# Gate-up matrices of the middle experts in 4 MB transfers instead of 2 MB ones

## The chip, the core and the metric

The kernel runs on one core of a Trainium2 chip. The metric is the device time of one launch in microseconds (us). TensorE (PE) multiplies, VectorE (DVE) and ScalarE (ACT) do the element-wise work, GpSimd (POOL) some set-up, and SyncE (SP) issues nearly all transfers. The transfers run on the core's 16 DMA engines: each takes 8 of the 128 partitions' rows of a transfer, and a semaphore tells the consumer when all 16 are through.

## The reference

One step of a hybrid decoder: a mixer, then a mixture of 32 experts, of which each of the 264 tokens (256 of a prompt, 8 samples) uses 4. All data are float32. What matters here is the expert part:

```
def expert_block(args):
    tok, e = args
    xb = x_pad[tok]
    h = jnp.einsum('rd,df->rf', xb, w_gate_up[e]) + b_gate_up[e]
    gate = jnp.minimum(h[:, :D_FF], SWIGLU_LIMIT)
    up = jnp.clip(h[:, D_FF:], -SWIGLU_LIMIT, SWIGLU_LIMIT)
    glu = gate * jax.nn.sigmoid(gate * SWIGLU_ALPHA)
    return jnp.einsum('rf,fd->rd', (up + 1.0) * glu, w_down[e]) + b_down[e]
```

`w_gate_up[e]` is 1024 x 2048 (8 MB), `w_down[e]` is 1024 x 1024 (4 MB). Every weight is used once, so the 32 experts bring 403 MB through the DMA engines.

## The kernel before

The launch has two stages. The mixer takes roughly the first 290 us. After it come the experts, in 16 pairs, each expert with room for 64 tokens, so that the two experts of a pair share the PE's 128 columns or rows.

The weights go through a ring of 8 slots of 2 MB in SBUF (16 KB a partition), `ring` (slots 0 to 5) and `late_ring` (slots 6 and 7, whose memory is the mixer's until its end). One slot holds one chunk: a quarter of a gate-up matrix (256 rows, two neighbouring rows of 8 KB in each partition, i.e. one piece of 16 KB a partition) or half a down matrix (four neighbouring rows of 4 KB a partition, also 16 KB). The order of the chunks is a fixed list for each pair of experts. With the chunks numbered from 0:

- `HEAD`, chunks 0 to 7: gate-up of experts 0 and 1.
- `BODY`, 14 times, 12 chunks each (the first is 8 to 19, the second 20 to 31): four of gate-up of the pair's first expert, four of the down matrices of the pair before, four of gate-up of the second expert. In the texts they are c0 to c11 of a body; c4 to c7 are the down ones.
- `LAST`, chunks 176 to 191: eight gate-up chunks and eight of down, the last ones loaded in pieces of 1 MB and 512 KB.

SP walks through this list. Ahead of chunk n it waits until PE has used chunk n-8, whose slot it takes (`used`, L555), and issues the load (`load_chunk`, L467 to L489). The load adds 16 to the semaphore of its slot (`expert_in`) when it has landed. PE waits for that semaphore ahead of each gate-up chunk (L915), works on it and then adds 1 to `used` (L928); for the down chunks it waits for two slots at once (L944) and adds 2 at the end (L955). PE has other work between the chunks: it gathers the tokens of the next pair (L1006), turns the hidden values (L994) and scatters results (L1035, L1036). All of this is in program order on PE, so PE's wait for one chunk holds up everything behind it.

Which rows of the gate-up matrix lie in which partition is chosen by the rearrangement of `gu_w` (L441). The gathered tokens have to lie in the same order (`gather`, L1004 to L1008, steps through the columns of `normed` by 2) and so do the norm weights (`ffn_pairs`, L603).

Of the kernel before, what the change touches and what calls it, by code (L numbers as in the profile page):

```python
# [37 lines left out]
P = 128  # L38
# [170 lines left out]
def build(nc, ins, outs):  # L209
# [4 lines left out]
    with ExitStack() as ctx:  # L214
        def sem(name):
            return ctx.enter_context(nc.semaphore(name))
# [158 lines left out]
        state_in = [sem(f"state_in{s}") for s in range(4)]  # L375
        state_out = [sem(f"state_out{s}") for s in range(4)]
        expert_in = [sem(f"expert_in{s}") for s in range(RING)]
        stored, y_out = sem("stored"), sem("y_out")
        cleared, sq_done, rms_done, rstd_ready, rstd_turned, rstd_row_ready = (
            sem(n) for n in ("cleared", "sq_done", "rms_done", "rstd_ready", "rstd_turned", "rstd_row_ready"))  # L380
# [57 lines left out]
        TILES = ((0, P), (P, P), (2 * P, NS))  # L438


        gu_w = ins["w_gate_up"].rearrange("l e (k p i) f -> (l e) p k (i f)", p=P, i=2)  # L441

        dn_w = ins["w_down"].rearrange("l e (k p i) f -> (l e) p k (i f)", p=P, i=4)

# [8 lines left out]
        def chunk_number(r, chunks, p, c):  # L453

            if chunks is HEAD:
                return PASS * r + c
            return PASS * r + len(BODY) * (p - 1) + len(HEAD) + c

        def chunk_there(r, chunks, p, c, b=0):

            before = c if chunks is HEAD else len(HEAD) + b * len(BODY) + c
            whole = 16 * (PASS // RING) * r + 16 * (before // RING + 1)
            if chunks is HEAD:
                return whole
            return whole + 16 * len(BODY) // RING * (p - b - 1)

        def load_chunk(sp, chunks, p, c, b=0):  # L467

            j, part, k = chunks[c]
            s = chunk_slot(chunks, c, b)  # L470
            if part == "gu":
                e = 2 * (0 if chunks is HEAD else p) + j
                src = gu_w[bass.ds(e, 1), :, k, :].rearrange("a p f -> p (a f)")
                sp.dma_start(slot(s), src).then_inc(expert_in[s], 16)
                return
            e, h = 2 * (p - 1 + j) + k % 2, k // 2
            if chunks is not LAST:
                src = dn_w[bass.ds(e, 1), :, h, :].rearrange("a p f -> p (a f)")
                sp.dma_start(slot(s), src).then_inc(expert_in[s], 16)
                return  # L480


            final = c == len(LAST) - 1
            for i, n in [(i, 1) for i in range(4)] if final else ((0, 2), (2, 2)):
                for x in range(2):
                    to = chunk_slot(chunks, c - 1 + x, b)
                    src = dn_w[bass.ds(e - 1 + x, 1), :, h, i * D:(i + n) * D].rearrange("a p f -> p (a f)")
                    sp.dma_start(slot(to)[:, i * D:(i + n) * D], src).then_inc(
                        expert_in[to] if i == 0 else last_in[i - 1] if final else later_in[2 * j + h], 16)  # L489
# [4 lines left out]
        @block.sync  # L494
        def _(sp):
            w_in = ins["w_in"].rearrange("l (k p) n -> p (l k) n", p=P)
            w_pb = ins["w_pool_branch"].rearrange("l (k p) n -> p (l k) n", p=P)
            w_ret = ins["w_ret_branch"].rearrange("l (k p) n -> p (l k) n", p=P)
            w_out = ins["w_out"].rearrange("l (k p) n -> p (l k) n", p=P)

            for t in range(2):
                sp.dma_start(tok[:, t, :], x_prompt[0, t * P:(t + 1) * P, :]).then_inc(x_in[t], 16)
            sp.wait_ge(cleared, 2)
            sp.dma_start(tok[0:NS, 2, :], x_sample.rearrange("b s d -> (b s) d")).then_inc(x_in[2], 16)
            sp.dma_start(tok[NS:NS + NM, 2, :], meta).then_inc(x_in[2], 16)

            def mix_chunk(i):
                kind, c = CHUNKS[i]
                s = i % MIX_SLOTS
                if i >= MIX_SLOTS:  # L510
                    sp.wait_ge(tile_done, last_tile(i - MIX_SLOTS) + 1)
                dst = unit(8 + s)
                if kind == "in":
                    cols = PROJ[c] * P
                    src = w_in[:, :, cols:cols + 2 * P]
                    dst = dst.rearrange("p (k n) -> p k n", k=KD)
                elif kind == "pb":
                    src = w_pb[:, :, c * 512:c * 512 + 512]
                    dst = dst.rearrange("p (k n) -> p k n", k=PG)
                else:  # L520
                    src = (w_ret if kind == "ret" else w_out)[:, :, c * 256:c * 256 + 256]
                    dst = dst.rearrange("p (k n) -> p k n", k=KD)
                sp.dma_start(dst, src).then_inc(wmix_in[s], 16)

            for i in range(C_PB):
                mix_chunk(i)
                if i == 1:
                    sp.dma_start(mix_consts[:, :], ins["consts"][:, N_KEPT:]).then_inc(consts_in, 16)
                    sp.dma_start(consts[:, EARLY:], ins["consts"][:, EARLY:N_KEPT]).then_inc(consts_in, 16)
                if i in (MIX_SLOTS + 3, MIX_SLOTS + 5):  # L530
                    load_chunk(sp, HEAD, None, (i - MIX_SLOTS - 3) // 2)

            sp.wait_ge(o_s_ready, 1)
            for s in range(4):
                sp.wait_ge(state_out[s], 32)
            sp.wait_ge(stored, 16 * 3)
            for s in range(2, 4):
                load_chunk(sp, HEAD, None, s)
            for i in range(C_PB, len(CHUNKS)):
                mix_chunk(i)  # L540

            sp.wait_ge(dve_took, T_OUT - T_YB)
            for s in range(RING_EARLY, RING):
                load_chunk(sp, HEAD, None, s)
            for s in range(2):
                sp.wait_ge(tile_done, last_tile(len(CHUNKS) - MIX_SLOTS + 2 * s + 1) + 1)
                load_chunk(sp, HEAD, None, 4 + s)

            def stream(r, chunks, p, b=0):

                for c in range(len(chunks)):
                    if chunks is LAST and chunks[c][1] == "dn" and chunks[c][2] % 2 == 0:

                        continue
                    sp.wait_ge(used, chunk_number(r, chunks, p, c) - RING + 1)  # L555
                    load_chunk(sp, chunks, p, c, b)

            with sp.Fori(1, NPAIR - 1, 2) as p:
                for b in range(2):
                    stream(0, BODY, p + b, b)  # L560
            sp.wait_ge(passes_ready, 1)
            passes = sp.value_load(passes_i[0:1, 0:1], min_val=1, max_val=NPASS)
            stream(0, LAST, NPAIR - 1)
            with sp.If(passes > 1):
                with sp.Fori(1, NPASS) as r:
                    with sp.If(passes > r):
                        stream(r, HEAD, None)
                        with sp.Fori(1, NPAIR - 1, 2) as p:
                            for b in range(2):
                                stream(r, BODY, p + b, b)  # L570
                        stream(r, LAST, NPAIR - 1)
            sp.wait_ge(y_first_ready, 1)
            sp.dma_start(y_prompt[0, 0:P, :], normed[:, 0, :]).then_inc(y_out, 16)
            sp.wait_ge(y_s_ready, 1)
            sp.dma_start(y_sample.rearrange("b s d -> (b s) d"), normed[0:NS, 2, :]).then_inc(y_out, 16)
            sp.wait_ge(y_out, 16 * 3)
            sp.wait_ge(stored, 16 * 3)
            sp.wait_ge(ret_out, 16)
            for s in range(4):
                sp.wait_ge(state_out[s], 32)  # L580
# [3 lines left out]
        def _(pool):  # L584
# [12 lines left out]
            for b in range(4):  # L597
# [2 lines left out]
            pool.dma_start(w_router, ins["w_router"].rearrange("l (k p) e -> p (l k) e", p=P)).then_inc(misc_in, 16)  # L600
            pool.dma_start(b_router[:, :], ins["b_router"].broadcast_to([P, NE])).then_inc(misc_in, 16)

            pool.dma_start(ffn_pairs.rearrange("p (k i) -> p k i", i=2),  # L603
                           ins["norm_ffn"].rearrange("l (k p i) -> p (l k) i", p=P, i=2)).then_inc(ffn_in, 16)
            pool.dma_start(pool_sample[0, :, 0:PBUF - 1, :], state_pool[0, :, 1:PBUF, :]).then_inc(stored, 16)


# [66 lines left out]
        def _(pe):  # L674
# [228 lines left out]
            def use_gate_up(r, chunks, p, c, j, half, b=0):  # L903
# [4 lines left out]
                if half == 0:  # L908
                    if k % 2 == 0:
# [2 lines left out]
                            pe.wait_ge(x_second_ready, 2 * r + 1 + k // 2)  # L912
                        else:
                            pe.wait_ge(x_ready, 2 * GATHERS * r + e + 1 + j + k // 2)
                    pe.wait_ge(expert_in[s], chunk_there(r, chunks, p, c, b))  # L915

                order = [(i, n) for n in range(2) for i in range(2)] if k == KC - 1 else [(i, n) for i in range(2)
                                                                                          for n in range(2)]
# [79 lines left out]
            def gather(r, g, half, bank, part=None):  # L998
# [2 lines left out]
                if half == 0 and part != 1:  # L1001
                    pe.wait_ge(one_hot_ready, GATHERS * r + g + 1)
                for k in blocks:
                    d0 = k // 2 * 2 * P + k % 2  # L1004
                    for t in range(3):
                        last = mm(psum[:, bank + half, (k % 4) * P:(k % 4 + 1) * P],  # L1006
                                  normed[:, t, d0:d0 - k % 2 + 2 * P:2],
                                  one_hot[:, t].rearrange("p j c -> p (j c)"), start=t == 0, stop=t == 2)  # L1008
                if part != 0:
                    last.then_inc(gathered, 1)  # L1010
# [823 lines left out]
```

## Time and profile before

| | us |
|---|---|
| median of three runs | 1229.53 (1227.49 to 1230.05) |
| span of the profiled execution | 1228.2 |
| PE busy | 1184.3 (96%) |
| DVE / ACT / POOL busy | 291.6 / 144.8 / 46.3 |

The profiled execution is given by its span, the time from its first to its last instruction. It lies 1.3 us under the median of the runs. The page's slices show three stretches. Up to about 300 us the DMA engines carry 80 to 313 GB/s. From 340 us on they carry 384 to 431 GB/s, busy in every slice, until shortly before the end. The PE row is at 9 tenths nearly everywhere; this busy time includes the tails of overlapping matmuls and says little on slack, so the waits are read from the other views.

### The profile page before, as it was taken

The page shows a single profiled execution, that of the slowest core. Times are in us where ns is not written, and L with a number is a line of the kernel's source. Part 1 is how long each engine was busy: PE and PEld are TensorE (multiplying, and loading weights), DVE is VectorE, ACT ScalarE, POOL GpSimd, SP SyncE. Part 2 cuts the span into 40 slices and gives each one's busy share as a digit, 9 for nine tenths or more (in the row PEclk, how much of TensorE's full clock was granted, in tenths as well). Part 3 has the DMA queues.
Part 4 walks back from the last instruction along what each step waited for, and adds up shares of the span by engine and source line. Part 5 has one row for each costly group of instructions (what it writes and reads, how often), then busy time and mean ns, then how long its engine had stood idle before and what let it go on. Part 6 is the DMA issues. An engine that isn't in the chain of part 4 may idle for free.

```text
span 1228.2 us, 14689 instructions
## 1 busy us (share of the span) xinstructions
PE 1184.3 (96%) x5910; PEld 624.1 (51%) x5910; DVE 291.6 (24%) x663; ACT 144.8 (12%) x288; POOL 46.3 (4%) x82
## 2 busy tenths in 40 slices
PE   8999999999999999999989999999998999999996
PEld 6888678877443444444434434343443444444432
DVE  2233311223122122121213221223121222212212
ACT  2122111002101101000101010010100000000112
POOL 3023310000000000000000000000000000000000
PEclk9999999999999999999989999999998999999999
DMA  9752776474999999999999999999999999999995
GB/s 313 243 206 80 250 251 225 138 274 154 414 384 418 429 428 427 429 429 429 427 429 429 429 429 429 428 428 427 427 429 427 431 428 429 429 427 430 427 419 207
DMA packets 65886, 450.85 MB, mean 367 GB/s; under 512 B 4433, under 2 KB 35453, under 8 KB 40752
## 3 DMA queue, kind: packets, MB, share of 16 engines
q1 hardware_dynamic: 62416, 438.95, 86.6%
q0 software_dynamic: 3088, 10.77, 2.7%
q8 instruction: 27, 0.44, 0.1%
q10 hardware_dynamic: 344, 0.61, 0.1%
q14 instruction: 11, 0.09, 0.0%
HBM read 444.46 MB, written 6.08 MB: 367 GB/s over the span
## 4 chain that ended last, share of the span: by engine, by line
PE 70%; DMA 27%; DVE 1%; SPq 1%; issue 0%; ACT 0%; POOL 0%; DVEq 0%; POOLq 0%
DMA ring<-in_w_down 26%; PE psum L923 20%; PE psum L934 18%; PE psum L858 18%; PE psum L1006 5%; PE psum L994 2%; DMA ring<-in_w_in 2%; PE psum L1035 1%; PE psum L1036 1%; PE psum L741 0%; PE psum L1023 0%; PE psum L756 0%; PE psum L879 0%; PE psum L924 0%; DVE normed L1782 0%
## 5 line engine op out<-in xcount | busy, mean ns | idle before, releaser
L923 PE MATMUL psum<-ring,x_T 128*64 128x512 f32 x768 | 350.1, 599 | 0.6 <-DVE x_T L1612 0.3
L924 PE MATMUL psum<-ring,x_T 128*64 128x512 f32 x768 | 350.1, 599 | 0.0
L934 PE MATMUL psum<-ring,act_T 128*64 128x512 f32 x736 | 176.5, 634 | 24.7 <-DMA ring<-in_w_down 24.7
L923 PEld LDWEIGHTS psum<-ring,x_T 128*64 128x64 f32 x768 | 99.5, 137 | 190.8 <-issue 180.3
L858 PE MATMUL psum<-u_T,ring 128*128 128x264 f32 (+1 forms) x704 | 167.7, 393 | 2.0 <-DVE u_T L1492 1.2
L858 PEld LDWEIGHTS psum<-u_T,ring 128*128 128x128 f32 x704 | 131.0, 190 | 30.0 <-issue 4.8
L1705 DVE TENSOR_TENSOR hg<-psum,params 128x512 f32<-128x512 f32 x32 | 22.1, 691 | 436.7 <-PE psum L994 436.7
L934 PEld LDWEIGHTS psum<-ring,act_T 128*64 128x64 f32 x736 | 57.7, 145 | 126.5 <-issue 123.4
L1006 PEld LDWEIGHTS psum<-one_hot,normed 128*128 128x128 f32 x816 | 101.0, 196 | 39.2 <-issue 38.3
L923 PE MATMUL psum<-late_ring,x_T 128*64 128x512 f32 x256 | 118.2, 600 | 0.0
L924 PE MATMUL psum<-late_ring,x_T 128*64 128x512 f32 x256 | 118.2, 600 | 0.0
L1006 PE MATMUL psum<-one_hot,normed 128*128 128x128 f32 x816 | 111.2, 287 | 0.6 <-DVE one_hot L1592 0.6
L924 PEld LDWEIGHTS psum<-ring,x_T 128*64 128x64 f32 x768 | 99.5, 137 | 0.0
L1722 DVE TENSOR_TENSOR z_T<-z_T,psum 128x264 f32<-128x264 f32 x120 | 46.4, 425 | 126.9 <-PE psum L1036 122.1
L1297 ACT COPY h_raw<-psum 128x512 f32<-128x512 f32 x32 | 18.8, 587 | 379.9 <-PE psum L924 379.9
L923 PEld LDWEIGHTS psum<-late_ring,x_T 128*64 128x64 f32 x256 | 31.9, 136 | 56.5 <-issue 51.5
L1303 ACT ACTIVATE hs<-hg 128x512 f32<-128x512 f32 x32 | 20.2, 630 | 290.3 <-DVE hg L1708 290.3
L934 PE MATMUL psum<-late_ring,act_T 128*64 128x512 f32 x224 | 49.6, 595 | 0.0
L994 PEld LDWEIGHTS psum<-consts,h_raw 128*128 128x128 f32 x256 | 33.3, 209 | 26.4 <-issue 26.0
L1035 PEld LDWEIGHTS psum<-hot_T,out_hi 128*128 128x128 f32 x112 | 21.0, 187 | 45.4 <-issue 45.4
L1717 DVE SCALAR_TENSOR_TENSOR act_T<-hu,hs 128x512 f32<-128x512 f32 x30 | 20.8, 692 | 83.3 <-PE psum L934 76.7
L994 PE MATMUL psum<-consts,h_raw 128*128 128x128 f32 x256 | 39.8, 297 | 0.0
(265 smaller groups left out, 811.7 us busy)
## 6 DMA issues: line engine op xcount, KB each, us to landing
ring<-in_w_gate_up SPq DMA_DIRECT2D x96, 2048.0 KB, 27.3
ring<-in_w_down SPq DMA_DIRECT2D x42, 2048.0 KB, 31.1
late_ring<-in_w_gate_up SPq DMA_DIRECT2D x32, 2048.0 KB, 28.5
late_ring<-in_w_down SPq DMA_DIRECT2D x14, 2048.0 KB, 31.6
ring<-in_w_in SPq DMA_DIRECT2D x22, 1024.0 KB, 5.7
ring<-in_w_down SPq DMA_DIRECT2D x12, 1024.0 KB, 28.2
ring<-in_state_ret POOLq DMA_DIRECT2D x8, 512.0 KB, 7.4
out<-ring POOLq DMA_DIRECT2D x8, 512.0 KB, 4.5
```

The lines of the kernel that those rows point to most:

```text
L858: last = mm(o[:, 0:width], w[:, k, cols:cols + P], x[:, k, 0:width], start=k == 0, stop=k == nk - 1)
L923: mm(psum[0:CAP, 2 * j + n], x, gate, start=first, stop=final)
L924: last = mm(psum[CAP:P, 2 * j + n], x, up, start=first, stop=final)
L934: last = mm(psum[j * CAP:(j + 1) * CAP, 4 + n], hidden[:, j, 4 * h + i], w, start=h == 0 and i == 0, stop=h == 1 and i == 3)
L994: last = pe.transpose(psum[:, 6 + m // 4, (m % 4) * P:(m % 4 + 1) * P], h_raw[:, j, f0:f0 - m % 4 + 4 * P:4], ident)
L1006: last = mm(psum[:, bank + half, (k % 4) * P:(k % 4 + 1) * P], normed[:, t, d0:d0 - k % 2 + 2 * P:2], one_hot[:, t].rearrange("p j c -> p ...
L1035: mm(o, out_hi[:, c], hot_T[:, :], start=True, stop=False)
L1297: nc.scalar.copy(h_raw[:, j, 0:512], psum[:, 2 * j]).then_inc(raw_ready, 1)
L1303: A(hs[:, :, :], hg[:, :, :], ACT.Silu, scale=ALPHA).then_inc(silu_ready, 1)
L1705: V.tensor_tensor(hg, turned[:, :, 0], bias(e, 0), ALU.add).then_inc(gate_biased, 1)
L1717: V.scalar_tensor_tensor(hidden[:, j], hu, 1.0, hs, ALU.add, ALU.mult).then_inc(act_ready, 1)
L1722: V.tensor_tensor(y_T[:, d], y_T[:, d], psum[:, 6 + d % 2, 0:NT], ALU.add).then_inc(y_added, 1)
```

## The change

The gate-up chunks of the 14 bodies are loaded two at a time, except the first two. A transfer now has 4 MB, with four neighbouring rows (32 KB) in each partition, and fills two neighbouring slots. It is issued when PE has used both chunks that lay there before, and has one semaphore for the two slots (`pair_in`). PE waits for it ahead of the first chunk of the two and not ahead of the second. Of the 112 gate-up chunks in the bodies, 110 go in 55 such transfers; chunks 8 and 9 go in two 2 MB transfers into one `pair_in`. `HEAD`, `LAST` and the down matrices keep their transfers. Since the rows lie in another order, a gate-up chunk of `HEAD`, of `LAST` and chunks 8 and 9 are now pieces of 16 KB with a pitch of 32 KB in HBM; the gather steps by 4 columns instead of 2, and the norm weights follow. On SP the first two bodies now stand outside the loop.

```diff
@@ -375,6 +375,7 @@
         state_in = [sem(f"state_in{s}") for s in range(4)]
         state_out = [sem(f"state_out{s}") for s in range(4)]
         expert_in = [sem(f"expert_in{s}") for s in range(RING)]
+        pair_in = [sem(f"pair_in{q}") for q in range(RING // 2)]
             sem(n) for n in ("cleared", "sq_done", "rms_done", "rstd_ready", "rstd_turned", "rstd_row_ready"))
@@ -438,7 +439,7 @@
-        gu_w = ins["w_gate_up"].rearrange("l e (k p i) f -> (l e) p k (i f)", p=P, i=2)
+        gu_w = ins["w_gate_up"].rearrange("l e (k p i) f -> (l e) p k (i f)", p=P, i=4)
@@ -456,13 +457,34 @@
                 return PASS * r + c
             return PASS * r + len(BODY) * (p - 1) + len(HEAD) + c
+        TWO_BODIES = (NPAIR - 2) // 2
         def chunk_there(r, chunks, p, c, b=0):
-            before = c if chunks is HEAD else len(HEAD) + b * len(BODY) + c
-            whole = 16 * (PASS // RING) * r + 16 * (before // RING + 1)
+            before = 16 * (1 + TWO_BODIES + 2) * r
             if chunks is HEAD:
-                return whole
-            return whole + 16 * len(BODY) // RING * (p - b - 1)
+                return before + 16
+            if chunks is LAST:
+                return before + 16 * (1 + TWO_BODIES + 1 + c // RING)
+            return before + 32 + 8 * (p - b - 1)
+        def pair_there(r, p, c, b):
+            again = 1 if chunk_slot(BODY, c, b) == 0 else 0
+            return 16 * 2 * TWO_BODIES * r + 16 * (1 + BODY[c][0] + again) + 16 * (p - b - 1)
+        def slots_of_pair(s):
+            return ring[:, s * SLOT:(s + 2) * SLOT] if s < RING_EARLY else late_ring[:, (s - RING_EARLY) * SLOT:(s - RING_EARLY + 2) * SLOT]
+        def gate_up_rows(e, k):
+            return gu_w[bass.ds(e, 1), :, k // 2, k % 2 * SLOT:(k % 2 + 1) * SLOT].rearrange("a p f -> p (a f)")
+        def load_pair(sp, p, c, b):
+            j, _, k = BODY[c]
+            s = chunk_slot(BODY, c, b)
+            src = gu_w[bass.ds(2 * p + j, 1), :, k // 2, :].rearrange("a p f -> p (a f)")
+            sp.dma_start(slots_of_pair(s), src).then_inc(pair_in[s // 2], 16)
         def load_chunk(sp, chunks, p, c, b=0):
@@ -470,8 +492,7 @@
             if part == "gu":
                 e = 2 * (0 if chunks is HEAD else p) + j
-                src = gu_w[bass.ds(e, 1), :, k, :].rearrange("a p f -> p (a f)")
-                sp.dma_start(slot(s), src).then_inc(expert_in[s], 16)
+                sp.dma_start(slot(s), gate_up_rows(e, k)).then_inc(expert_in[s], 16)
                 return
             if chunks is not LAST:
@@ -552,10 +573,31 @@
                     if chunks is LAST and chunks[c][1] == "dn" and chunks[c][2] % 2 == 0:
+                    if chunks is BODY and chunks[c][1] == "gu":
+                        if chunks[c][2] % 2 == 0:
+                            sp.wait_ge(used, chunk_number(r, chunks, p, c + 1) - RING + 1)
+                            load_pair(sp, p, c, b)
+                        continue
-            with sp.Fori(1, NPAIR - 1, 2) as p:
+            def first_pair():
+                for c in range(2):
+                    sp.wait_ge(used, chunk_number(0, BODY, 1, c) - RING + 1)
+                    sp.dma_start(slot(c), gate_up_rows(2, c)).then_inc(pair_in[0], 16)
+            first_pair()
+            for c in range(2, len(BODY)):
+                if BODY[c][1] == "dn":
+                    sp.wait_ge(used, chunk_number(0, BODY, 1, c) - RING + 1)
+                    load_chunk(sp, BODY, 1, c)
+                elif BODY[c][2] % 2 == 0:
+                    sp.wait_ge(used, chunk_number(0, BODY, 1, c + 1) - RING + 1)
+                    load_pair(sp, 1, c, 0)
+            stream(0, BODY, 2, 1)
+            with sp.Fori(3, NPAIR - 1, 2) as p:
                 for b in range(2):
@@ -600,8 +642,8 @@
-            pool.dma_start(ffn_pairs.rearrange("p (k i) -> p k i", i=2),
-                           ins["norm_ffn"].rearrange("l (k p i) -> p (l k) i", p=P, i=2)).then_inc(ffn_in, 16)
+            pool.dma_start(ffn_pairs.rearrange("p (k i) -> p k i", i=4),
+                           ins["norm_ffn"].rearrange("l (k p i) -> p (l k) i", p=P, i=4)).then_inc(ffn_in, 16)
@@ -912,7 +954,10 @@
-                    pe.wait_ge(expert_in[s], chunk_there(r, chunks, p, c, b))
+                    if chunks is not BODY:
+                        pe.wait_ge(expert_in[s], chunk_there(r, chunks, p, c, b))
+                    elif k % 2 == 0:
+                        pe.wait_ge(pair_in[s // 2], pair_there(r, p, c, b))
                 order = [(i, n) for n in range(2) for i in range(2)] if k == KC - 1 else [(i, n) for i in range(2)
                                                                                           for n in range(2)]
@@ -1001,10 +1046,10 @@
                 if half == 0 and part != 1:
                 for k in blocks:
-                    d0 = k // 2 * 2 * P + k % 2
+                    d0 = k // 4 * 4 * P + k % 4
                     for t in range(3):
-                                  normed[:, t, d0:d0 - k % 2 + 2 * P:2],
+                                  normed[:, t, d0:d0 - k % 4 + 4 * P:4],
                 if part != 0:
```

SP, the load of c8 to c11 of a body inside the loop, before. `used` is the wait for the slot, `128x4096` is 16 KB a partition:

```order
L474 ISA [waits used]
L474 DMA ring<-in_w_gate_up 128x4096
L555 REGISTER_ALU
L474 ISA [waits used]
L474 DMA ring<-in_w_gate_up 128x4096
L555 REGISTER_ALU
L474 ISA [waits used]
L474 DMA late_ring<-in_w_gate_up 128x4096
L555 REGISTER_ALU
L474 ISA [waits used]
L474 DMA late_ring<-in_w_gate_up 128x4096
L555 REGISTER_ALU
```

The same place now. `128x8192` is 32 KB a partition:

```order
L487 ISA [waits used]
L487 DMA ring<-in_w_gate_up 128x8192
L579 REGISTER_ALU
L487 ISA [waits used]
L487 DMA late_ring<-in_w_gate_up 128x8192
L582 REGISTER_ALU
```

Four waits and four loads have become two and two. Each wait is now for the later of the two chunks whose slots are taken.

PE, first body, from the last matmuls of c8 into c9 (`expert_in1` is the semaphore of c9's slot), before:

```order
L924 MATMUL psum<-ring,x_T 64x512
L923 MATMUL psum<-ring,x_T 64x512
L924 MATMUL psum<-ring,x_T 64x512
L923 MATMUL psum<-ring,x_T 64x512 [waits hidden_took,expert_in1,out_split,hot_ready]
L924 MATMUL psum<-ring,x_T 64x512
L923 MATMUL psum<-ring,x_T 64x512
L924 MATMUL psum<-ring,x_T 64x512
```

The same place now:

```order
L969 MATMUL psum<-ring,x_T 64x512
L968 MATMUL psum<-ring,x_T 64x512
L969 MATMUL psum<-ring,x_T 64x512
L968 MATMUL psum<-ring,x_T 64x512 [waits hidden_took,out_split,hot_ready]
L969 MATMUL psum<-ring,x_T 64x512
L968 MATMUL psum<-ring,x_T 64x512
L969 MATMUL psum<-ring,x_T 64x512
```

The wait for the second chunk's own load is gone; the other waits of that instruction stay. PE, the same body, from the scatter inside c9 into c10, before:

```order
L1030 REGISTER_ALU
L1035 MATMUL psum<-hot_T,out_hi 128x264 [waits y_added]
L1036 MATMUL psum<-hot_T,out_lo 128x264
L1030 REGISTER_ALU
L1035 MATMUL psum<-hot_T,out_hi 128x264 [waits y_added]
L1036 MATMUL psum<-hot_T,out_lo 128x264
L923 MATMUL psum<-ring,x_T 64x512 [waits expert_in2,x_ready]
L924 MATMUL psum<-ring,x_T 64x512
L923 MATMUL psum<-ring,x_T 64x512
```

The same place now:

```order
L1075 REGISTER_ALU
L1080 MATMUL psum<-hot_T,out_hi 128x264 [waits y_added]
L1081 MATMUL psum<-hot_T,out_lo 128x264
L1075 REGISTER_ALU
L1080 MATMUL psum<-hot_T,out_hi 128x264 [waits y_added]
L1081 MATMUL psum<-hot_T,out_lo 128x264
L968 MATMUL psum<-ring,x_T 64x512 [waits pair_in1,x_ready]
L969 MATMUL psum<-ring,x_T 64x512
L968 MATMUL psum<-ring,x_T 64x512
```

Ahead of c10 PE now waits for `pair_in1`, the landing of c10 and c11 together; its line number moved with the diff and its work is the same.

## Rows read from the trace of the kernel before

**Rows 1.** windows: busy us (count) by engine, PEclk, DMA share, GB/s.

```profile
400.00:1130.00 730.00, 706.42 (x3500) 305.67 (x3499) 161.42 (x332) 67.77 (x127) 0.00 (x0) 0.98 1.01 428
1176.00:1196.00 20.00, 18.29 (x92) 7.16 (x90) 2.65 (x5) 3.14 (x5) 0.00 (x0) 1.00 1.01 421
1202.00:1208.00 6.00, 6.00 (x26) 2.40 (x25) 0.00 (x0) 0.00 (x0) 0.00 (x0) 1.00 1.02 408
```

**Rows 2.** critical chain: start us, length us, what; 394 to 503 us.

```profile
393.95 1.16 PE psum L994 x8
...
502.31 1.16 PE psum L994 x8
```

**Rows 3.** the same chain, 868 to 1112 us.

```profile
868.75 7.09 PE psum L934 x32
...
1044.93 8.78 PE psum L934 x32
...
1071.51 32.01 DMA ring<-in_w_down
1103.65 8.48 PE psum L934 x32
```

**Rows 4.** waits, 540 to 1130 us: total us, times, longest.

```profile
PE psum L934 <- DMA ring<-in_w_down: 23.0, 9, 4.0
```

**Rows 5.** one line (L474): its DMAs, issue to landing.

```profile
DMA to landing us min/median/max: 7.6/27.7/35.3
```

**Rows 6.** SP by time, 300 to 400 us: start, length, issues.

```profile
300.74 3.76 SPq L474 DMA_DIRECT2D ring<-in_w_gate_up  x2
...
311.42 3.77 SPq L474 DMA_DIRECT2D ring<-in_w_gate_up  x2
...
319.88 3.80 SPq L479 DMA_DIRECT2D ring<-in_w_down  x2
...
329.93 6.92 SPq L479 DMA_DIRECT2D late_ring<-in_w_down  x2
...
339.96 5.06 SPq L474 DMA_DIRECT2D ring<-in_w_gate_up  x2
...
355.08 0.33 SPq L474 DMA_DIRECT2D ring<-in_w_gate_up  x1
...
363.74 0.92 SPq L474 DMA_DIRECT2D ring<-in_w_gate_up  x2
...
373.62 0.91 SPq L474 DMA_DIRECT2D late_ring<-in_w_gate_up  x2
```

**Rows 7.** windows, 326 to 420 us.

```profile
326.00:360.00 34.00, 34.00 (x184) 16.12 (x184) 5.82 (x12) 2.98 (x5) 0.00 (x0) 1.00 1.00 421
...
362.00:364.00 2.00, 2.00 (x12) 0.83 (x9) 0.00 (x0) 0.00 (x0) 0.00 (x0) 1.00 0.39 164
```

**Rows 8.** SP by time, 1124 us on.

```profile
1125.52 4.59 SPq L474 DMA_DIRECT2D ring<-in_w_gate_up  x2
```

**Rows 9.** PE by time, 1186 to 1200 us; in brackets idle before.

```profile
1188.65 3.65 PE L934 MATMUL psum<-ring,act_T 128*64 128x512 f32 x16 [0.44 <-DMA ring<-in_w_down]
1193.53 3.65 PE L934 MATMUL psum<-ring,act_T 128*64 128x512 f32 x16 [1.23 <-DMA ring<-in_w_down]
1198.69 1.90 PE L934 MATMUL psum<-ring,out_sq 128*64 128x512 f32 x7 [1.50 <-DMA ring<-in_w_down]
```

**Rows 10.** windows: PE after its wait at 1103 us.

```profile
1103.00:1106.00 3.00, 2.35 (x6) 0.86 (x8) 0.00 (x0) 0.00 (x0) 0.00 (x0) 0.51 1.00 426
...
1186.00:1200.00 14.00, 10.83 (x53) 3.65 (x51) 1.50 (x2) 1.37 (x2) 0.00 (x0) 1.00 1.01 418
```

**Rows 11.** PE by time, 1103 us.

```profile
1103.65 1.98 PE L934 MATMUL psum<-ring,act_T 128*64 128x512 f32 x4 [2.78 <-DMA ring<-in_w_down]
```

**Rows 12.** groups of PEld (weight loads) by line, 540 to 1130 us.

```profile
L1006 PEld LDWEIGHTS psum<-one_hot,normed 128*128 128x128 f32 x480 | 59.7, 196 | 24.3 <-issue 24.3
L994 PEld LDWEIGHTS psum<-consts,h_raw 128*128 128x128 f32 x160 | 20.7, 209 | 16.2 <-issue 16.2
```

## The prediction

> **What bounds the kernel now.** I read the page's slices first, then windows of the expert stage, the chain of waits, and the issues of SP at the stage's start. The slices show that PE is at 9 tenths nearly everywhere and that the DMA engines are at 9 tenths from 340 us on, so busy shares don't decide. A window of 400 to 1130 us gives 428 GB/s with the DMA engines full [rows 1]. The chain decides. Early bodies are paced by PE: from 393.95 to 502.31 us two bodies pass, 54.18 us each, without a DMA in the chain [rows 2]. Later ones are paced by transfers: the first down matmuls of a body start at 868.75 and, four bodies on, at 1103.65, which is 58.72 us a body or 4.894 us a chunk (2.097 MB, so 428.5 GB/s) [rows 3]. PE could do a body in 54.2 us, so it waits: 23.0 us in nine waits between 540 and 1130 us, nearly all for a down chunk [rows 4]. So the end is set by this sum: when the stream of chunks starts, the time in which its queue is dry, bytes over rate, and the tail behind the last landing. PE matters only where it frees slots too late, or where it is late itself at the end.
>
> **Part 1: half the transfers for 110 chunks.** Every transfer costs something besides its bytes. From the rate by size of row [rows 1]: rows of 8 KB (1 MB a transfer) run at 421 GB/s, 2.491 us each, twice that is 4.981; less the 4.894 of one 2 MB transfer that leaves 0.087 us per transfer saved. Rows of 4 KB (512 KB) run at 408 GB/s, 1.285 us each, four are 5.140, less 4.894 leaves 0.246 for three, 0.082 each. I take 0.08. The change saves 55 of these, 4.4 us; five of the 55 fall into the start, counted in part 2, so 50 x 0.08 = 4.0 us here. Bounds: nothing is saved if the engines cut a 32 KB row in two (no row of the trace is that long in this queue); the most is 55 x 0.09 = 5.0 us.
>
> The Trainium skill (DMA: Bandwidth & Descriptors, "Anatomy of one DMA — SWDGE (gpsimd) path") gives a transfer 2.0 us fixed plus its bytes at 436 GB/s; were that paid in the queue, 55 fewer would save 110 us. The trace disagrees: it would make a body of twelve chunks 82 us, and it is 58.7 [rows 3]. The fixed part shows only where the queue is dry, as the 2.7 us of part 2. The same page ("Why small descriptors are slow (HBM only)") speaks of about 3 cycles per packet; by our estimate from its 850 MHz that is 28 ns for the eight packets of an engine, 1.5 us for 55 transfers, against 4.4 by the rows, and the sum would end near 1229.3.
>
> **Part 2: at the start the pairs come later.** Here SP is held by PE: the queue is nearly dry while PE uses chunks 0 to 15. A load issued into a dry queue lands after 7.6 us [rows 5], that is 4.9 of its own and 2.7 before. So I replay with: landing = the later of (landing before it + own time) and (issue + 2.7 + own time). Own time is 4.89, for a pair 9.71 (9.79 - 0.08). Issue times stand in [rows 6], where the last of a row's issues is start + length - 0.33. The slots' release by PE is the same, but a pair is issued at the later of its two times.
> Before: chunks 8 and 9 (issued 300.74, 304.16) land at 308.3, 313.2; 10 (311.42) at 319.0; 11 to 14 every 4.89 to 338.6; 15 (336.51) at 344.1; 16 to 19 to 363.7; 20 (363.74) at 371.3, so the queue is dry for 2.7 us, seen as 164 GB/s in the window from 362 us [rows 7]; 21 at 376.2; 22 and 23 (373.62) at 381.2 and 386.1.
> Now: 8 and 9 the same; 10 and 11 issued together at 314.85, landing 327.3 (before 323.9); 12 to 15 at 346.9; 16 and 17 issued at 344.69, landing 357.1; 18 and 19 at 355.08, landing 367.5; 20 and 21 at 363.74, queued, landing 377.2; 22 and 23 landing 386.9.
> That is 0.8 us later than before. The dry 2.7 us at 362 us absorb most of it. Other traffic holds the stream at 421 instead of 428.5 GB/s from 326 to 360 us [rows 7], 34 x 0.018 = 0.6 us; before it hid in part in dry time, now it has less to hide in. So +0.8 to +1.4 us, and I take 1.3. Later no pair is late: loads land a median 27.7 us after issue [rows 5], over five chunks, and a pair gives up one chunk of that. PE has chunks in hand throughout this stretch (chunk 10 is used after 344.69), so it isn't held.
>
> **Part 3: PE waits for two chunks where it waited for one.** Behind each such wait stand all of PE's gathers, turns and scatters, then ACT and DVE, and SP's next loads. While PE is 4.5 us a body ahead this only moves the waits: now it waits up to about 2 us ahead of c8, c10, c0 and c2, and reaches the down chunks late by about what it would have waited. It counts only in the last body, whose end PE carries into the tail. There, c9 ends at 1129.8 (1125.52 + 4.59 - 0.33) [rows 8]. The first down chunks of that body had landed at 1103.52 (1071.51 + 32.01) [rows 3]; c11 lands six chunks on, at 1132.9, and with the gain of parts 1 and 2 at 1130.2. So c10 starts 0.4 us later than before. From there PE has slack 0.44 + 1.23 + 1.50 = 3.2 us, its waits ahead of the last down pieces [rows 9]; less the 0.4 that is 2.8 us. After the last of these waits PE runs through to its end. So the gain can't pass 3.2 us whatever the DMA engines save, and 2.8 is my value for this limit.
>
> **Part 4: the rest.** The gather reads weights with a step of 4 columns. A weight load with step 2 is 196 ns, the step-4 loads of L994 are 209 [rows 12]; at worst 13 ns x 48 = 0.6 us of PE a body, hidden by its 4.5 us, and 0.3 us in the last expert's 24 gathers; if the two operands explain the difference, nothing or a little less. I take 0. Rows of 16 KB at a pitch of 32 KB for the 18 single gate-up chunks in `HEAD`, `LAST` and the first body: no row shows this; I take 0, and 1% of 18 x 4.9 us would be 0.9 either way. SP issues 55 fewer; each is 0.33 us under a queue that is full, so 0. The norm weights' load is far ahead of its use, 0.
>
> **Sum.** DMA: -4.0 + 1.3 = -2.7 us. PE's limit: -2.8. So 1228.2 becomes 1225.5 as a profile. The median of the runs is 1.3 above that profile: 1229.53 - 2.7 = 1226.8 us.
>
> **Rivals.**
> A, the row is cut: the engines move 32 KB as two packets and pay per packet. Then only the coarser start is left, +1.3, and 55 semaphores saved at most 0.5: 1230.4. For it: the saving in part 1 is read from smaller rows, and no row excludes it. Against: the rule held from 4 to 16 KB with one constant.
> B, PE's clock: after a wait of 2.78 us [rows 11] the granted clock fell to the lower level, 1.2 GHz (0.51 in the window from 1103) [rows 10], and the 32 down matmuls took 8.5 to 8.8 us instead of 7.1 [rows 3], 1.5 to 1.7 us. Waits of 0.44 to 1.50 did not do this: clock 1.00 from 1186 to 1200 [rows 10]. The new waits of about 2 us lie between. If both in the last body (c8, c10) cost 1.7, PE is 3.4 later, over its 2.8 of slack by 0.6, and instead of the gain the end is at 1229.5 - 2.7 + 3.4 - 0.1 = 1230.1. One such loss gives about 1228.4.
> C, slower: 32 KB rows run slower. Each engine then reads longer rows, 32 KB apart instead of 16. Place: all 110 chunks, 538 us. From 0.5% on (428.5 down to 426.3 GB/s, a pair over 9.84 us) it eats the 2.7; at 1% it costs 5.4 on top of the start's 1.3: 1236.2. For it: nothing shown, rates rise with the row (408, 421, 428). That rise is what speaks against it.
>
> **Numbers.** Forecast 0.66, A 0.13, B 0.12, C 0.09. About 0.2% (2.5 us) is what a measurement of this kernel can tell from no change. The forecast's own spread is 1225.3 (limit of PE, one us of scatter) to 1228.3 (0.05 per transfer, start 1.7), so it lies half over that bound: 0.43 of its 0.66 is faster, 0.22 the same, 0.01 slower. A and B are the same mostly, with 0.04 faster and 0.03 slower between them, C slower or the same. Together faster 0.47, same 0.42, slower 0.11. The range is 1225.0 to 1230.7: it holds A and B and leaves C out.
>
> **What would show it.** In the profile after: 55 gate-up issues of 4096 KB; down starts later than 700 us spaced 58.4 us (58.72 - 4 x 0.08) instead of 58.72, the clearest sign for part 1 (58.7 would be A, more would be C); no 164 GB/s slice at 362 us; PE's waits for `in_w_gate_up` no longer near zero, about the same total; waits ahead of the last down pieces near 0.5 us in total instead of 3.2. I am wrong if the spacing doesn't shrink, if the queue goes dry beyond 390 us, or if the spacing shrinks and the end does not follow.

## The result: 4.5% slower

| kernel | median us (lowest to highest) | ratio to before, 95% interval |
|---|---|---|
| before | 1229.79 (1227.49 to 1230.77), 4 runs | |
| changed | 1284.12 (1282.75 to 1286.19), 4 runs | 1.0447 (1.0435 to 1.0460) |

The forecast was 1226.8 us. The changed kernel is 54 us slower. The head of its page gives the profiled execution:

```profile
span 1282.5 us, 14402 instructions
PE 1264.3 (99%) x5910; PEld 711.7 (55%) x5910; DVE 292.9 (23%) x663; ACT 146.0 (11%) x288; POOL 46.2 (4%) x82
```

PE was 96% busy and is now 99% busy, with 80 us more busy time in the same number of matmuls (5910). The answers to [rows 4], PE's waits from 300 us to the end (total us, times, longest):

```profile
PE psum L979 <- DVE out_lo L1731: 0.8, 1, 0.8
PE psum L968 <- DVE x_T L1657: 0.3, 1, 0.3
```

Not one of PE's waits is for a transfer. They were 23.0 us in the middle stretch alone. So the bound has changed sides: the transfers wait for PE. The window that answers to the first of [rows 1] (engines as there):

```profile
400.00:1130.00 730.00, 729.85 (x3344) 352.91 (x3344) 158.56 (x325) 66.04 (x121) 0.00 (x0) 1.00 0.99 417
```

PE is busy for 729.85 of 730 us and the transfers run at 417 instead of 428 GB/s, because slots come free later. The issues by line, with the size and the median us from issue to landing, show that the transfers arrive sooner after their issue than before, not later:

```profile
ring<-in_w_gate_up SPq DMA_DIRECT2D x41, 4096.0 KB, 14.7
...
late_ring<-in_w_gate_up SPq DMA_DIRECT2D x14, 4096.0 KB, 14.5
```

There are 55 transfers of 4096 KB, as intended, and a landing takes 14.7 us where a single chunk took 27.7 [rows 5]: the queue is short. The chain, by the first of each body's turns of the hidden values (L1039 is L994 before; start, length):

```profile
410.00 1.16 PE psum L1039 x8
...
469.72 1.16 PE psum L1039 x8
...
529.43 1.16 PE psum L1039 x8
```

A body takes 59.7 us, all of it PE. It was 54.18 us where PE paced it and 58.72 where the transfers did [rows 2, 3]. Where the 5.5 us come from stands in the groups of PE's weight loads, which answer to [rows 12] (us busy, mean ns | idle before):

```profile
L1051 PEld LDWEIGHTS psum<-one_hot,normed 128*128 128x128 f32 x816 | 195.1, 329 | 39.2 <-issue 38.3 <-DVE one_hot L1637 0.9
...
L1039 PEld LDWEIGHTS psum<-consts,h_raw 128*128 128x128 f32 x256 | 33.3, 209 | 26.4 <-issue 26.0 <-ACT h_raw L1344 0.4
```

and in the matmuls of the same line, now:

```profile
L1051 PE MATMUL psum<-one_hot,normed 128*128 128x128 f32 x816 | 205.3, 403 | 0.6 <-DVE one_hot L1637 0.6
```

before:

```profile
L1006 PE MATMUL psum<-one_hot,normed 128*128 128x128 f32 x816 | 111.2, 287 | 0.6 <-DVE one_hot L1592 0.6
```

The gather's weight loads take 329 ns instead of 196, its matmuls 403 instead of 287. There are 48 of each in a body: 48 x 0.116 = 5.6 us. The turns' loads, whose step is 4 in both kernels, have not moved. The 133 ns between the two loads are more than PE pays, since the records of neighbouring loads overlap: the 816 loads are busy for 195.1 us now, 239 ns each, and were busy for 101.0 us, 124 ns each, which is 115 ns apart. The chain says the same. Twelve matmuls of the gather, before and now:

```profile
398.70 1.61 PE psum L1006 x12
```

```profile
414.75 3.00 PE psum L1051 x12
```

That is 1.39 us for twelve, 0.116 each. Below, the lengths of loads are given as the profile has them; what PE pays is read from the chain.

The 54 us are not 14 bodies at 5.5 us. The first down matmuls of the first, the fourth and (now) the last body, before and now (the last one before is at 1103.65 in [rows 3]):

```profile
356.51 7.02 PE psum L934 x32
...
519.05 7.02 PE psum L934 x32
```

```profile
371.19 7.02 PE psum L979 x32
...
550.33 7.02 PE psum L979 x32
...
1155.45 7.02 PE psum L979 x32
```

14.7 us are lost ahead of the first body's down matmuls, 16.6 in the three bodies behind them, which PE paced before too, and 20.5 in the last ten; 2.5 us come behind them. In the bodies that the transfers had paced at 58.7 us a body loses only about 1.0. Eight of the 20.5 us are one block on PE that both kernels have: 16 matmuls of the biases with short waits for DVE between them (5.8 us from 824 us on, L1078) and, behind them, about four us at the lower clock, 1.2 GHz (granted 0.50 from 828 to 832 us). Before, the body with this block took 62.6 us and the next one 54.9, so the two passed in the time of the transfers; now nothing takes it up.

### The profile page after: what moved, and what is told of

Its sections match the earlier page's. It is cut to its first block, busy times and chain, and to the rows that moved or that the text cites. A ratio compares the mean times of both kernels' runs of the same rounds, so it can differ in the third digit from the quotient of the medians.

```text
span 1282.5 us, 14402 instructions
## 1 busy us (share of the span) xinstructions
PE 1264.3 (99%) x5910; PEld 711.7 (55%) x5910; DVE 292.9 (23%) x663; ACT 146.0 (11%) x288; POOL 46.2 (4%) x82
## 4 chain that ended last, share of the span: by engine, by line
PE 97%; DVE 1%; ACT 0%; issue 0%; DVEq 0%
PE psum L968 35%; PE psum L900 18%; PE psum L979 17%; PE psum L1051 16%; PE psum L1039 3%; PE psum L1080 2%; PE psum L1081 1%; PE psum L969 1%; PE psum L1068 0%; PE psum L783 0%; PE psum L1078 0%; PE psum L798 0%; DVE normed L1827 0%; PE psum L771 0%; PE psum L770 0%; PE psum L762 0%
## 5 line engine op out<-in xcount | busy, mean ns | idle before, releaser
L1051 PEld LDWEIGHTS psum<-one_hot,normed 128*128 128x128 f32 x816 | 195.1, 329 | 39.2 <-issue 38.3
L1051 PE MATMUL psum<-one_hot,normed 128*128 128x128 f32 x816 | 205.3, 403 | 0.6 <-DVE one_hot L1637 0.6
L979 PE MATMUL psum<-ring,act_T 128*64 128x512 f32 x736 | 163.2, 596 | 0.0
L979 PEld LDWEIGHTS psum<-ring,act_T 128*64 128x64 f32 x736 | 50.8, 137 | 94.7 <-issue 92.9
L1767 DVE TENSOR_TENSOR z_T<-z_T,psum 128x264 f32<-128x264 f32 x120 | 46.5, 426 | 127.9 <-PE psum L1081 122.1
L1039 PEld LDWEIGHTS psum<-consts,h_raw 128*128 128x128 f32 x256 | 33.3, 209 | 26.4 <-issue 26.0
L1039 PE MATMUL psum<-consts,h_raw 128*128 128x128 f32 x256 | 39.8, 297 | 0.0
## 6 DMA issues: line engine op xcount, KB each, us to landing
ring<-in_w_gate_up SPq DMA_DIRECT2D x41, 4096.0 KB, 14.7
```

Source lines behind the costliest of these rows:

```text
L979: last = mm(psum[j * CAP:(j + 1) * CAP, 4 + n], hidden[:, j, 4 * h + i], w, start=h == 0 and i == 0, stop=h == 1 and i == 3)
L1039: last = pe.transpose(psum[:, 6 + m // 4, (m % 4) * P:(m % 4 + 1) * P], h_raw[:, j, f0:f0 - m % 4 + 4 * P:4], ident)
L1767: V.tensor_tensor(y_T[:, d], y_T[:, d], psum[:, 6 + d % 2, 0:NT], ALU.add).then_inc(y_added, 1)
```

## The experiments

Theory G: the loss is the gather, whose weight loads read the tokens with a step of 4 elements. Rival T: the loss is the 4 MB transfers, which come late or run slowly.

**The gather's step alone, in the kernel before.**

```diff
-                    d0 = k // 2 * 2 * P + k % 2
+                    d0 = k // 4 * 4 * P + k % 4
-                                  normed[:, t, d0:d0 - k % 2 + 2 * P:2],
+                                  normed[:, t, d0:d0 - k % 4 + 4 * P:4],
```

> The kernel before with one edit: the gather reads the tokens' columns with a step of 4 instead of 2. Rows and transfers stay as before, so the experts get the columns of each token in a wrong order; the work and its amount are the same. Theory G (the loss of 54 us is the gather's weight loads): the weight loads of the gather go from 196 to about 329 ns and its matmuls from 287 to about 403, a body takes PE about 59.9 us instead of 54.2, PE waits for no transfer, and the time is 1280 to 1288 us. Theory T (the loss is the 4 MB transfers, which come late): the time stays at 1228 to 1231 us.

Measured: 1285.30 us, ratio 1.0460 (1.0444 to 1.0476). The weight loads:

```profile
L1006 PEld LDWEIGHTS psum<-one_hot,normed 128*128 128x128 f32 x816 | 195.0, 328 | 39.2 <-issue 38.3 <-DVE one_hot L1592 0.9
...
L994 PEld LDWEIGHTS psum<-consts,h_raw 128*128 128x128 f32 x256 | 33.3, 209 | 26.4 <-issue 26.0 <-ACT h_raw L1299 0.4
```

PE's waits from 300 us on:

```profile
PE psum L934 <- DVE out_lo L1686: 0.8, 1, 0.8
PE psum L923 <- DVE x_T L1612: 0.3, 1, 0.3
```

This is the whole loss, with the transfers of before. Theory T falls.

**The changed kernel with the old step.** The same two lines the other way round.

> The changed kernel with one edit: the gather steps by 2 again, so the columns of each token are in a wrong order for its weight rows; everything else is as changed, with 55 transfers of 4 MB. Theory G: the gather's weight loads are back at 196 ns, PE waits for transfers again, and the time is what parts 1 and 2 of the prediction gave, 1225.5 to 1228.5 us, with 58.4 us a body where the transfers are the bound. Theory T: 1280 us or more. A mixed case, in which the coarse transfers cost something by themselves: 1230 to 1240 us.

Measured: 1225.83 us, ratio 0.9973 (0.9962 to 0.9983), faster than before. PE's waits from 300 us on:

```profile
PE psum L968 <- DMA ring<-in_w_gate_up: 26.1, 21, 1.7
PE psum L968 <- DMA late_ring<-in_w_gate_up: 6.1, 6, 1.1
PE psum L979 <- DVE out_lo L1731: 0.9, 1, 0.9
```

PE waits for transfers again, but in 27 short waits of at most 1.7 us ahead of gate-up pairs instead of a dozen up to 4.0 us ahead of down chunks: part 3 of the prediction as it was written. Two bodies of its chain:

```profile
925.96 7.04 PE psum L979 x32
...
1042.83 7.04 PE psum L979 x32
```

That is 58.43 us a body, with the gather of before, against 58.73 for the same two bodies of the kernel before.

**Both orders with the tokens packed.** ACT writes each block of 128 columns densely; the gather then reads with step 1. In the changed kernel (the other has `h=4, i=2`):

```diff
-                A(normed[0:n, t], banks((4, 6, 0)[t], 2)[0:n], ACT.Copy, ...)
+                A(normed[0:n, t].rearrange("n (h i p) -> n h i p", h=2, i=4),
+                  banks((4, 6, 0)[t], 2)[0:n].rearrange("n (h p i) -> n h i p", h=2, i=4),
+                  ACT.Copy, ...)
...
-                                  normed[:, t, d0:d0 - k % 4 + 4 * P:4],
+                                  normed[:, t, k * P:(k + 1) * P],
```

> The changed kernel, but ACT writes the normalised tokens so that the 128 columns of one gather block lie next to each other (three instructions that read PSUM with a step of 4 and write densely), and the gather reads them with step 1. Outputs are the reference's. Theory G: weight loads of the gather at 190 ns or less, the time 1225.0 to 1228 us, under the kernel before. Theory T: 1280 us or more.

> The kernel before with the same packing of the normalised tokens, for its own order of rows (ACT reads PSUM with a step of 2), gather with step 1, 2 MB transfers. Outputs are the reference's. The transfers are its bound, so a slightly faster gather gives little: 1228 to 1230 us by both theories. It is the base against which after_packed shows what the 4 MB transfers are worth: theory of part 1 says after_packed is 2 to 3.5 us below it.

Measured: after_packed 1225.49 us, 0.9967 (0.9955 to 0.9979); before_packed 1229.00 us, 0.9998 (0.9989 to 1.0007). The gather's loads in after_packed:

```profile
L1050 PEld LDWEIGHTS psum<-one_hot,normed 128*128 128x128 f32 x816 | 95.9, 192 | 39.2 <-issue 38.3 <-DVE one_hot L1638 0.9
```

The chain of after_packed, the first down matmuls of three bodies:

```profile
925.48 7.04 PE psum L979 x32
...
984.00 7.04 PE psum L979 x32
...
1042.33 7.04 PE psum L979 x32
```

and of before_packed:

```profile
926.66 9.53 PE psum L934 x32
...
985.38 8.78 PE psum L934 x32
...
1044.13 8.78 PE psum L934 x32
```

That is 58.43 us a body (116.85 for two) against 58.74 (117.47): four pairs save 0.31 us, 0.08 us each, the price of part 1. The transfers of after_packed in the same window as above:

```profile
400.00:1130.00 730.00, 696.93 (x3499) 298.13 (x3497) 162.33 (x334) 67.69 (x127) 0.00 (x0) 0.99 1.00 431
```

431 GB/s, where the kernel before has 428.

**The order of the rows with single transfers.**

```diff
-                src = gu_w[bass.ds(e, 1), :, k, :].rearrange("a p f -> p (a f)")
+                src = gu_w[bass.ds(e, 1), :, k // 2, k % 2 * SLOT:(k % 2 + 1) * SLOT].rearrange("a p f -> p (a f)")
```

on the packed kernel in the new order (`i=4` in `gu_w` and `ffn_pairs`).

> Rows in the new order (four neighbouring rows a partition), but every gate-up chunk in its own 2 MB transfer of 16 KB pieces at a pitch of 32 KB; the tokens packed, gather with step 1. Outputs are the reference's. If the gain of after_packed over before_packed (3.5 us) comes from fewer, longer transfers (the 0.08 us per transfer of part 1), this kernel is at 1228 to 1230 us with 58.7 us a body. If it came from the order of the rows itself, it is at 1225 to 1226 us. If pieces at a 32 KB pitch were slower by 1%, it would be at 1234 us.

Measured: 1227.44 us, 0.9987 (0.9978 to 0.9996). Its bodies:

```profile
925.29 9.83 PE psum L934 x32
...
984.02 7.09 PE psum L934 x32
...
1042.75 8.78 PE psum L934 x32
```

58.73 us on average, as with the old order, so pieces of 16 KB at a pitch of 32 KB are not slower. That its median lay 1.6 us under before was not expected, so the three were run again side by side:

> The packed kernel with the old order of rows and 2 MB transfers once more, on one chip with the next two, since the gains of order_2mb_packed (ratio 0.9987) and before_packed (0.9998) were measured in different calls. Expected 0.9995 to 1.0000 of the kernel before: its body is paced by transfers at 58.7 us.

> The new order of rows with 2 MB transfers once more. If the order of the rows is worth nothing, it equals before_packed_again within 0.1%; if it is worth the 1.6 us seen, it lies 1 us or more below it.

> The new order of rows with 55 transfers of 4 MB once more. If the fewer transfers are what gains (0.3 us a body, 58.4 instead of 58.7), it lies 2 to 4 us below both others; if the order of rows carries half of it, 1 to 2 us below order_2mb_packed_again.

Measured: 1228.26 us, 0.9995 (0.9986 to 1.0004); 1227.49 us, 0.9989 (0.9980 to 0.9998); 1224.28 us, 0.9967 (0.9955 to 0.9979). The 4 MB transfers are worth 3.2 to 4.0 us against the other two. Between the first two lie 0.8 us (1.6 in the runs before), with overlapping intervals and bodies of the same length. The new order came out lower both times; whether the order of the rows is itself worth this much stays open.

**How the price depends on the step.** The kernel before with step 3 and step 8 in the gather (`d0 = k * 64` and `d0:d0 + 3 * P:3`; `d0 = k` and `d0:D:8`).

> The kernel before with the gather's weight loads at step 3 (384 columns of which every third is read; data wrong, amount of work the same). Theory L (a load slows by the number of 16-byte lines it touches per element: 1 element per line is slow, 2 and more are not): step 3 has 4 elements in 3 lines, so the load lies between 196 (step 2) and 329 ns (step 4), about 240 to 290. If it is a threshold at step 4: 196. If any step over 2 is slow: 329.

> The kernel before with the gather's weight loads at step 8 (data wrong). Theory L: every element is in a line of its own from step 4 on, so the load stays at about 329 ns and the time at about 1285 us. If the cost grows with the bytes passed over: about 600 ns and well over 1350 us.

Measured, one run each: 1237.09 and 1287.11 us. The loads at step 3:

```profile
L1006 PEld LDWEIGHTS psum<-one_hot,normed 128*128 128x128 f32 x816 | 146.5, 260 | 39.2 <-issue 38.3 <-DVE one_hot L1592 0.9
```

and at step 8:

```profile
L1006 PEld LDWEIGHTS psum<-one_hot,normed 128*128 128x128 f32 x816 | 198.7, 333 | 39.2 <-issue 38.3 <-DVE one_hot L1592 0.9
```

With 192 ns at step 1 (after_packed), 196 at step 2 and 328 at step 4, the series is 192, 196, 260, 328, 333. The Trainium skill (SBUF — State Buffer, "Specifications (TRN2)") gives SBUF lines of 16 bytes, of which an access has to hit each at least twice to run at full speed. By 4-byte elements the steps 1, 2, 3, 4 and 8 touch 1/4, 1/2, 3/4, 1 and 1 line per element, and the measured series agrees: step 2 has two hits a line, step 4 one. So a load is nearly free of the step up to half a line per element, and from one line on it no longer grows. At step 3, PE hardly waits for transfers (total us, times, longest):

```profile
PE psum L934 <- DMA ring<-in_w_down: 2.6, 2, 1.5
```

The first turns of two bodies in its chain:

```profile
402.07 1.16 PE psum L994 x8
...
458.93 1.16 PE psum L994 x8
```

A body takes PE 56.86 us, 2.7 us more than at step 2 (48 x 0.056, by the matmuls, whose mean is 343 ns). That is less than the 4.5 us by which PE was ahead, and still the launch is 8 us longer (1237.09 against 1229.06). The landings in the two traces say where it is lost: the first down chunk of the second body, number 24, lands at 399.8 instead of 393.9 us, and from there to the end the transfers stay 6 to 8 us behind. In that first stretch SP waits for PE to free the slots, so there PE's time is not covered.

**Why L994 misled.** The turns of the hidden values as plain matmuls, and in another kernel the turns with step 1:

```diff
-                    last = pe.transpose(psum[...], h_raw[:, j, f0:f0 - m % 4 + 4 * P:4], ident)
+                    last = mm(psum[...], h_raw[:, j, f0:f0 - m % 4 + 4 * P:4], ident, start=True, stop=True)
```

```diff
-                                        h_raw[:, j, f0:f0 - m % 4 + 4 * P:4], ident)
+                                        h_raw[:, j, m * P:(m + 1) * P], ident)
```

> The kernel before, with the eight turns of the hidden values per expert (L994, step 4 in h_raw) as plain float32 matmuls against the identity instead of transposes. This is why the 209 ns of L994 misled the prediction: in transposes a step-1 load is 143 ns (L1023), so step 4 adds 66, and in plain matmuls step 1 is 190. If the price of step 4 belongs to the plain form, the loads of L994 go from 209 to about 329 ns. If it depends on the tile that is read (h_raw against normed), they go to 190 to 210. The whole time stays near 1230 us, since PE has slack there.

> The kernel before, with the turns of L994 reading h_raw with step 1 (data wrong). If the step was the reason for 209 ns, the loads of L994 fall to about 143 ns, the value of other transposes with step 1. If not, they stay at 209. The time stays at 1228 to 1230 us, transfers being the bound.

Measured, one run each: turn_plain 1275.57 us, turn_step1 1228.33 us. Weight loads of turn_plain:

```profile
L994 PEld LDWEIGHTS psum<-consts,h_raw 128*128 128x128 f32 x512 | 121.9, 328 | 26.0 <-issue 26.0
```

and of turn_step1:

```profile
L994 PEld LDWEIGHTS psum<-consts,h_raw 128*128 128x128 f32 x256 | 27.4, 141 | 26.6 <-issue 26.0 <-ACT h_raw L1299 0.7
```

The same tile and the same step, 209 ns as a transpose and 328 as a plain matmul; with step 1 the transpose loads in 141. In the chain, the turns of one expert (eight blocks of 128 x 128) as plain matmuls and as transposes with step 1:

```profile
401.80 3.93 PE psum L994 x16
```

```profile
416.14 1.02 PE psum L994 x8
```

Eight transposes with step 4 take 1.16 us [rows 2]. So in PE's time step 4 costs a transpose (1.16 - 1.02) / 8, about 0.017 us, where it costs a matmul of the gather 0.116. A plain float32 matmul is moreover two loads and two matmuls (x512 where the transposes were x256), so each of the two pays for the step. The expectation for turn_plain had the load right and the time wrong: 46.5 us were lost because the count doubled too, which I had not reckoned with, and PE's slack of 4.5 us a body was gone.

## Why the prediction was wrong

**The step that failed is in part 4:** "A weight load with step 2 is 196 ns, the step-4 loads of L994 are 209; at worst 13 ns x 48 = 0.6 us of PE a body, hidden by its 4.5 us." The measured term is 133 ns in the load's record, 0.116 us of PE a matmul, and 5.5 us a body in the spacing of the chain: over the 4.5 us by which PE was ahead. PE paces every body at 59.7 us. The 209 ns are those of a transpose, the 196 those of a plain matmul; I compared across two kinds. The trace of before has step 1 for the same kind as L994 (gated values, dense):

```profile
L1023 PEld LDWEIGHTS psum<-consts,gated 128*128 128x128 f32 x48 | 5.8, 143 | 0.8 <-issue 0.8
```

143 against 209 ns says that the step does lengthen a load, by 66 ns, and that would have been the warning. It isn't the price either. In PE's time the 66 ns of a transpose are 17, by turn_step1, and 48 x 0.017 = 0.8 us would have looked covered as well; the gather, in the plain form, pays 116. Why the plain form pays so much more isn't shown. None of the rows that I read had a plain matmul with a step over 2, and one was needed.

The cover was wrong too. The 4.5 us a body are there only in the bodies that the transfers pace; 31 of the 54 us were lost before these. And step3_only, whose 2.7 us a body are well inside the 4.5, lost 8 us. So the term was mis-sized, and what was to hide it hides less than I said.

The rule of the Trainium skill quoted with the series above says the same of steps 2 and 4. It names no size. It was the rule against this change, and the prediction should have weighed it.

**Part 1 was right.** A transfer saved is worth 0.08 us: 58.43 against 58.74 us a body where the transfers are the bound. The engines move a 32 KB row as one packet, as the packet count of the changed kernel's page shows:

```profile
DMA packets 57965, 450.84 MB, mean 352 GB/s; under 512 B 3553, under 2 KB 34573, under 8 KB 39872
```

The page of before counts 65886. The difference is 7921, and 55 transfers fewer, of 128 rows and 16 semaphore packets each, are 7920. So rival A falls, and with 431 GB/s so does C, a slower rate.

**Part 2 was right in kind.** The windows of after_packed that answer to the 164 GB/s of [rows 7]:

```profile
360.00:362.00 2.00, 2.00 (x12) 0.49 (x8) 0.00 (x0) 0.00 (x0) 0.00 (x0) 1.00 1.20 508
362.00:364.00 2.00, 2.00 (x17) 1.85 (x16) 0.44 (x1) 0.00 (x0) 0.00 (x0) 1.00 0.76 328
364.00:366.00 2.00, 2.00 (x16) 1.26 (x16) 2.00 (x5) 0.79 (x2) 0.00 (x0) 1.00 1.09 459
```

The dry stretch at 362 us is mostly filled: 328 GB/s in the slice that had 164. For the size of the part the landings in the traces of after_step2 and of before can be compared, which have the same gather. The pair of chunks 22 and 23 lands at 389.2 us where chunk 23 had landed at 388.2, and the first down chunk behind it at 394.2 instead of 393.9. So the start cost 0.3 to 1.0 us, where 1.3 were forecast. By chunk 168, in the last body, the transfers are 3.2 us ahead: 3.5 us gained over 48 pairs, 0.07 each, which bears out part 1.

**Part 3 was right in kind; its limit was too low.** The waits moved from the down chunks to the gate-up pairs. The end of after_packed (PE by time):

```profile
1182.22 3.65 PE L979 MATMUL psum<-ring,act_T 128*64 128x512 f32 x16
...
1186.77 7.09 PE L979 MATMUL psum<-ring,act_T 128*64 128x512 f32 x32
...
1194.96 3.65 PE L979 MATMUL psum<-ring,out_sq 128*64 128x512 f32 x16 [1.10 <-DMA ring<-in_w_down]
```

Of the 3.2 us of waits ahead of the last down pieces [rows 9] only 1.10 are left there, and none in after_step2, where PE runs through to its end; 0.5 were forecast. The forecast for parts 1 to 3, -2.7 us, measured -3.4 (after_step2) to -4.5 us (after_packed_again) against before; the second contains the step-1 gather. Both pass the 3.2 us that I had called the most that is possible, and the 2.8 that I took. In after_step2 c11 lands at 1129.5 us, not at 1130.2, so c10 starts at 1129.7 us and not 0.4 us later than before: the 0.4 that I took off the 3.2 were not there. Rival B, a falling clock, is not seen: PEclk is 0.99 in the window of after_packed, and its down matmuls take 7.04 us in the chain above, where before some took 8.8.

So the mechanisms that I worked out were there, and together within 2 us of what I said. The edit that I cost at nothing, by its cover, decided. The chance of 0.11 for slower was for other causes; nothing in the rivals had the gather.

## What to carry to other kernels

Price an edit of an access pattern by a row of the same instruction in the same form, and by the time in the chain and not the length of a load's record. A cover counts only where the other side sets the pace: 4.5 us over 48 matmuls are 94 ns each, but 56 ns each (step 3) already cost 8 us. When a transfer is made coarser by another order of rows, every reader that has to follow the order changes its step: pack the data once where they are written (three ACT instructions here) and the transfer's gain stays. The version that does so, after_packed, beats the kernel before by 0.33% (0.9967, 0.9955 to 0.9979, the same in both sets of its runs).

## What the runs showed of the hardware

Weight loads of 128 columns in float32: 192, 196, 260, 328 and 333 ns for steps 1, 2, 3, 4 and 8 in plain matmuls; 141 and 209 ns for steps 1 and 4 in transposes. These are lengths of records that overlap. In the chain, twelve plain matmuls with their loads take 1.53, 1.61, 2.28, 3.00 and 3.05 us at these steps, and eight transposes 1.02 and 1.16 us. From step 4 to step 8 there is hardly a further price. The transfers of 32 KB a partition ran at 431 GB/s in a mixture with those of 16 KB, which alone ran at 428.
